# Router and output projection of a two-layer mixture-of-experts trunk: logits in pairs of tiles, the projection's last two tiles in chunk groups, earlier weight requests

## The reference

```
for i in range(2):
    hn = rms_norm(h, norm1_g[i])
    h = h + (rwkv7_time_mix(hn) if i == 0 else conformer_conv(hn))   # each ends in "@ w_o" or "@ w_pw2"
    hn = rms_norm(h, norm2_g[i])
    h = h + hierarchical_moe(hn)
return rms_norm(h, final_g)
```

## Time and profile before

| | us |
|---|---|
| median of 3 runs | 1295.0 (1292.39 to 1297.48) |
| the profiled execution | 1299.55 |
| its span | 1297.5 |
| TensorE busy | 1158.7 (89%) |
| VectorE busy | 526.2 (41%) |
| ScalarE busy | 397.9 (31%) |
| GpSimd busy | 241.0 (19%) |

### The profile page before, as it was taken

How to read it: one execution, slowest core, us unless ns; L and a number is a source line. 1 busy time by engine, 2 the same in 40 slices (tenths; PEclk the granted TensorE clock), 3 DMA queues, 4 the chain that set the end, 5 groups by cost and what they waited for, 6 DMA issues and landing times.

```text
span 1297.5 us, 29460 instructions
## 1 busy us (share of the span) xinstructions
PE 1158.7 (89%) x12654; PEld 626.1 (48%) x12654; DVE 526.2 (41%) x961; ACT 397.9 (31%) x773; POOL 241.0 (19%) x243
## 2 busy tenths in 40 slices
PE   5999999999999989899988877999999899987880
PEld 3355556555555645455544433444444555544440
DVE  6855554554554512411111104699943411111115
ACT  3334445344443322021111113466444111111112
POOL 2000000000000003222211110688801322221110
PEclk8999999999999989899998998999999999999896
DMA  5011101011013072899999976126201699999985
GB/s 167 3 52 60 32 27 53 14 47 39 19 55 134 5 264 82 348 406 424 423 425 427 425 314 260 65 97 278 95 1 38 244 376 424 426 424 427 426 341 218
DMA packets 50209, 271.95 MB, mean 210 GB/s; under 512 B 16386, under 2 KB 19586, under 8 KB 31648
## 3 DMA queue, kind: packets, MB, share of 16 engines
q1 hardware_dynamic: 38048, 240.67, 46.0%
q0 software_dynamic: 10880, 21.00, 4.3%
q10 hardware_dynamic: 1152, 8.39, 1.6%
HBM read 263.73 MB, written 23.07 MB: 221 GB/s over the span
## 4 chain that ended last, share of the span: by engine, by line
PE 62%; DMA 21%; DVE 8%; POOL 4%; issue 2%; ACT 2%; SPq 1%; POOLq 0%; ACTq 0%; DVEq 0%
DMA big<-in_moe_w_gate_up_dram 18%; PE psum L1247 14%; PE psum L820 10%; PE psum L1734 9%; PE psum L1409 6%; PE psum L833 4%; POOL big L1951 4%; DVE psum L2105 2%; PE psum L1979 2%; PE psum L1398 2%; DVE h L924 1%; PE psum L1527 1%; PE psum L799 1%; PE psum L1545 1%; DVE big L431 1%
## 5 line engine op out<-in xcount | busy, mean ns | idle before, releaser
L820 PE MATMUL psum<-big 128*64 128x256 f32 x1728 | 219.5, 399 | 40.9 <-DMA big<-in_moe_w_gate_up_dram 29.7
L1247 PE MATMUL psum<-big 128*128 128x512 f32 x384 | 192.7, 623 | 2.9 <-ACT big L1281 2.2
L820 PEld LDWEIGHTS psum<-big 128*64 128x64 f32 x1728 | 121.4, 141 | 124.1 <-DMA big<-in_moe_w_gate_up_dram 41.2
L895 DVE TENSOR_TENSOR big<-big,psum 128x128 f32<-128x128 f32 x64 | 18.4, 288 | 323.2 <-ACT big L861 323.2
L761 POOL DMA_INDIRECT chosen<-big x64 | 63.7, 995 | 347.0 <-ACT big L871 179.1
L733 POOL TENSOR_SCALAR big<-big 128x1024 f32<-128x1024 f32 x8 | 22.8, 2848 | 566.5 <-PE psum L458 566.4
L833 PE MATMUL psum<-big 128*64 128x512 f32 x512 | 120.9, 593 | 1.2 <-ACT big L866 1.2
L1734 PE MATMUL psum<-big 128*128 128x512 f32 x256 | 115.6, 605 | 0.8 <-ACT big L2074 0.8
L1979 PE MATMUL psum<-big,conv_w 128*128 128x512 f32 x256 | 110.4, 593 | 2.1 <-ACT big L411 1.2
L1951 POOL TENSOR_TENSOR big<-big 128x512 f32<-128x512 f32 x81 | 103.0, 1272 | 42.1 <-ACT big L2053 31.6
L1580 ACT COPY big<-psum 128x512 f32<-128x512 f32 (+1 forms) x112 | 68.3, 648 | 125.1 <-PE psum L1409 122.3
(11 more groups left out here) (260 smaller groups left out, 1341.4 us busy)
## 6 DMA issues: line engine op xcount, KB each, us to landing
big<-in_moe_w_gate_up_dram SPq DMA_DIRECT2D x54, 2048.0 KB, 27.7
big<-in_moe_w_down_dram SPq DMA_DIRECT2D x64, 1024.0 KB, 33.5
conv_w<-in_moe_w_gate_up_dram SPq DMA_DIRECT2D x10, 2048.0 KB, 32.9
big<-in_rwkv_w_rkv_dram SPq DMA_DIRECT2D x24, 512.0 KB, 4.2
conv_w<-in_conv_w_pw_dram SPq DMA_DIRECT2D x8, 1024.0 KB, 4.7
big<-chosen ACTq DMA_DIRECT2D x8, 1024.0 KB, 8.3
big<-in_rwkv_w_o_dram SPq DMA_DIRECT2D x4, 1024.0 KB, 9.1
rows<-big POOLq DMA_DIRECT2D x8, 512.0 KB, 6.0
```

What stands on the lines that cost most here:

```text
L820: last = nc.tensor.matmul(o[half * SLOTS:(half + 1) * SLOTS, 0:F_EXP].rearrange("p (u f) -> p u f", u=2), m.xT[e // 2 % 2][:, c, (e % 2) * ...
L1247: last = nc.tensor.matmul(bank[b], m.w[:, n, c, :], x[:, c, :], start=(c == 0), stop=(c == C - 1))
```

## The change

- **Logits in pairs.** `pe_logits` now takes two tiles at once. Tile 2p writes PSUM partitions 0 to 35 of bank 0, tile 2p+1 partitions 64 to 99 of bank 1, alternating chunk by chunk. Tile 3 goes this way too, and `pe_last_logits` is gone. ScalarE copies the logits of tiles 0, 1 and 2, and DVE those of tile 3. The order on TensorE is columns of tile 2, logits of pair 0, columns of tile 3, flips of pair 0, logits of pair 1, flips of pair 1.
- **Routing in pairs.** DVE runs the steps from scale and bias to the two best experts once for tiles 0 and 1 and once for tiles 2 and 3. The copy into `gl` is gone: the logits tile has four padding columns behind the group logits. The mask's two instructions are one.
- **Moved off DVE's chain.** The shifts for the gates stand behind the tables. Two of the four code products are made by ScalarE (three activations). The rounds are one reduction in place of two steps, and the `rank` update is the last step of `dve_tables`.
- **Rows.** `hn[2]` and `hn[3]` are scaled by ScalarE, between its columns of tile 3 and the copy of tile 2's logits. It also clears `x`. GpSimd scales tiles 0 and 1 and issues all four stores, and reads the rounds before it waits for the stores.
- **Output projection.** Tiles 2 and 3 run in three groups of chunks, (0, 1), (2 to 5) and (6, 7), each first for tile 2, then for tile 3. The columns of tiles 0 and 1 stand behind tile 2's second group. `mix_freed` tells SP when chunks 0 to 1 and 0 to 5 are no longer read.
- **Weight requests.** Layer 0 asks for expert 0's up part right behind expert 3, its down part at the first `mix_freed`, expert 1's up part at the second, and expert 1's down part at the end of the projection. Layer 1 asks for expert 2 at the second `mix_freed`.
- **Expert loop.** `take_rows` is one copy of 1024 columns in place of two of 512, and `pe_stay_busy` writes bank 0. Several semaphores are shared between layers.

```
+        FLIP_BANKS = (4, 6, 5, 7)
         N_LOGITS = N_GRP + N_EXP
 
-        def pe_logits(m, mixer, pe, t):
-
-            pe.wait_ge(m.hnT_ready.sem, m.hnT_ready.by(2 * t + 2))
-            if t == 0:
-                pe.wait_ge(m.params_in, 16 * m.n_params)
+        def logit_rows(t):
+            return slice((t % 2) * 64, (t % 2) * 64 + N_LOGITS)
+
+        def logit_columns(t):
+            return slice((t // 2) * P, (t // 2 + 1) * P)
+
+        def pe_logits(m, mixer, pe, pair):
+
+            if pair == 0:
+                pe.wait_ge(m.params_in.sem, m.params_in.by(16 * m.n_params))
                 pe.wait_ge(mixer.mixed, TT - 1)
-            if t >= 2:
-                pe.wait_ge(m.logitsT_ready.sem, m.logitsT_ready.by(t - 1))
+                pe.wait_ge(m.hnT_ready.sem, m.hnT_ready.by(4))
+            else:
+                pe.wait_ge(m.logitsT_ready.sem, m.logitsT_ready.by(2))
             for c in range(C):
-                last = nc.tensor.matmul(bank[LOGIT_BANKS[t]][0:N_LOGITS, 0:P], m.w_route[:, c, :],
-                                        m.hnT[:, c, t * P:(t + 1) * P], start=(c == 0), stop=(c == C - 1))
+                if pair and c in (0, C // 2):
+                    pe.wait_ge(m.hnT_ready.sem, m.hnT_ready.by(2 * TT - 1 if c == 0 else 2 * TT))
+                for t in (2 * pair, 2 * pair + 1):
+                    last = nc.tensor.matmul(bank[t % 2][logit_rows(t), 0:P], m.w_route[:, c, :],
+                                            m.hnT[:, c, t * P:(t + 1) * P], start=(c == 0), stop=(c == C - 1))
             last.then_inc(m.logitsT_in_psum.sem, 1)
...
+        def pe_flip_logits(m, mixer, pe, pair):
...
+                pe.wait_ge(m.hnT_ready.sem, m.hnT_ready.by(6))
+            pe.wait_ge(m.logitsT_ready.sem, m.logitsT_ready.by(2 * pair + 2))
+            for t in (2 * pair, 2 * pair + 1):
+                nc.tensor.transpose(bank[FLIP_BANKS[t]][:, 0:N_LOGITS], m.logitsT[logit_rows(t), logit_columns(t)],
+                                    ident[logit_rows(t), logit_rows(t)]).then_inc(m.logits_in_psum.sem, 1)
 
         def pe_route_last(m, mixer, pe):
 
             pe_norm_columns(m, pe, TT - 2)
             pe_logits(m, mixer, pe, 0)
+            pe_norm_columns(m, pe, TT - 1)
+            pe_flip_logits(m, mixer, pe, 0)
             pe_logits(m, mixer, pe, 1)
-            pe_norm_columns(m, pe, TT - 1)
-            pe_logits(m, mixer, pe, 2)
-            for t in range(TT - 1):
-                pe_flip_logits(m, mixer, pe, t)
-            pe_last_logits(m, pe)
+            pe_flip_logits(m, mixer, pe, 1)
...
+            act.wait_ge(m.rstd_step.sem, m.rstd_step.by(3 * TT))
+            for t in range(TT // 2, TT):
+                nc.scalar.activation(m.hn[t], m.hn[t], ACT.Copy, scale=m.rstd[:, t:t + 1]).then_inc(m.rows_scaled.sem, 1)
             logits(2)
+            act.wait_ge(m.squares.sem, m.squares.by(TT))
+            for b in range(2):
+                nc.scalar.activation(m.x[b].rearrange("p (c s) -> p c s", c=C), ones[:].unsqueeze(1).broadcast_to([P, C, P]),
+                                     ACT.Copy, scale=0.0).then_inc(m.exp_ready.sem, 1)
...
-            step(nc.vector.tensor_copy(m.gl[:, :, 0:N_GRP], m.logits[:, :, 0:N_GRP]))
...
+            def choose_experts(pair):
+                two, both = (2 * pair, 2 * pair + 1), slice(2 * pair, 2 * pair + 2)
+                dve.wait_ge(m.rstd_step.sem, m.rstd_step.by(3 * (2 * pair + 2)))
+                dve.wait_ge(m.logits_in_psum.sem, m.logits_in_psum.by(2 * pair + 2))
+                for t in two:
+                    last = nc.vector.scalar_tensor_tensor(out=m.logits[:, t, 0:n], in0=bank[FLIP_BANKS[t]][:, 0:n],
+                                                          scalar=m.rstd[:, t:t + 1], in1=m.b_route, op0=ALU.mult,
+                                                          op1=ALU.add)
+                step(last)
+                for t in two:
+                    last = nc.vector.max(m.gmax[:, t, :], m.logits[:, t, N_EXP:])
+                step(last)
+                for t in two:
+                    last = nc.vector.max_index(m.gidx[:, t, :].bitcast(u32), m.gmax[:, t, :], m.logits[:, t, N_EXP:])
+                step(last)
+                step(nc.vector.tensor_copy(m.gidx_f[:, both], m.gidx[:, both, 0].bitcast(u32)))
+                step(nc.vector.tensor_tensor(m.in_group[:, both, :], group_iota[:].unsqueeze(1).broadcast_to([P, 2, N_EXP]),
+                                             m.gidx_f[:, both].unsqueeze(2).broadcast_to([P, 2, N_EXP]), ALU.not_equal))
+                step(nc.vector.scalar_tensor_tensor(out=m.el[:, both, :], in0=m.in_group[:, both, :], scalar=-3.0e38,
+                                                    in1=m.logits[:, both, 0:N_EXP], op0=ALU.mult, op1=ALU.add))
+                if pair == 0:
+                    dve.wait_ge(m.logitsT_in_psum.sem, m.logitsT_in_psum.by(2))
+                    nc.vector.tensor_copy(m.logitsT[logit_rows(TT - 1), logit_columns(TT - 1)],
+                                          bank[1][logit_rows(TT - 1), 0:P]).then_inc(m.logitsT_ready.sem, 1)
+                for t in two:
+                    last = nc.vector.max(m.emax[:, t, :], m.el[:, t, :])
+                step(last)
+                for t in two:
+                    last = nc.vector.max_index(m.eidx[:, t, :].bitcast(u32), m.emax[:, t, :], m.el[:, t, :])
+                step(last)
+
+            for pair in range(2):
...
+                choose_experts(pair)
...
-            step(nc.vector.tensor_tensor(m.gexp, m.logits[:, :, 0:N_GRP], m.gmax[:, :, 0:1].broadcast_to([P, TT, N_GRP]),
-                                         ALU.subtract))
-            step(nc.vector.tensor_tensor(m.ediff, m.emax[:, :, 1], m.emax[:, :, 0], ALU.subtract))
-            assert st.n == GATES_SHIFTED
-
             rhs = m.route_rhs.rearrange("p (t k) n e -> p t k n e", k=2)
-            nc.vector.tensor_tensor(rhs[:, :, :, 0, :], m.pick, token_low[:, 0:2].unsqueeze(1).unsqueeze(3)
-                                    .broadcast_to([P, TT, 2, N_EXP]), ALU.mult)
-            nc.vector.tensor_scalar(rhs[:, :, :, 1, :], m.pick, token_low[:, 2:3], None, ALU.mult)
...
-            dve_slots(m, dve)
+            dve_slots(m, dve, 0, TT)
             dve.wait_ge(m.route, most)
-            step(nc.vector.tensor_scalar(m.over, round_starts[:], m.cmax, None, ALU.is_lt))
-            step(nc.vector.tensor_reduce(m.n_over, m.over, AX.X, ALU.add))
-            nc.vector.tensor_scalar(m.rounds.bitcast(i32), m.n_over, 1.0, None, ALU.add).then_inc(m.rounds_ready, 1)
+            begun = st.done(nc.vector.tensor_scalar(m.over, round_starts[:], m.cmax, None, ALU.is_lt))
+            dve_slots(m, dve, TT, TT * 2)
+            dve.wait_ge(m.route, begun)
+            with nc.allow_low_precision("a count of at most eight rounds"):
+                nc.vector.tensor_reduce(m.rounds.bitcast(i32), m.over, AX.X, ALU.add).then_inc(m.rounds_ready, 1)
             dve_tables(m, dve, 0)
...
+            step(nc.vector.tensor_tensor(m.gexp, m.logits[:, :, groups], m.gmax[:, :, 0:1].broadcast_to([P, TT, N_GRP]),
+                                         ALU.subtract))
+            step(nc.vector.tensor_tensor(m.ediff, m.emax[:, :, 1], m.emax[:, :, 0], ALU.subtract))
+            assert st.n == GATES_SHIFTED
+            dve.wait_ge(m.exp_ready.sem, m.exp_ready.by(ACT_ROUTE))
...
+            rhs = m.route_rhs.rearrange("p (t k) n e -> p t k n e", k=2)
+            act.wait_ge(m.route, PICKED)
+            for k in range(2):
+                nc.scalar.activation(rhs[:, :, k, 0, :], m.pick[:, :, k, :], ACT.Copy, scale=token_low[:, k:k + 1])
+            nc.scalar.activation(rhs[:, :, :, 1, :], m.pick, ACT.Copy, scale=token_low[:, 2:3]
+                                 ).then_inc(m.exp_ready.sem, 1)
...
-            dve.wait_ge(m.hot_ready, TT * 2 * (r + 1))
-            nc.vector.tensor_scalar(m.rank, m.rank, -float(SLOTS), None, ALU.add).then_inc(m.slot_step, 1)
-            dve.wait_ge(m.slot_step, S * r + 1)
...
+            dve.wait_ge(m.hot_ready, TT * 2 * (r + 1))
+            nc.vector.tensor_scalar(m.rank, m.rank, -float(SLOTS), None, ALU.add).then_inc(m.slot_step, 1)
+            dve.wait_ge(m.slot_step, S * r + TABLE_STEPS)
...
+                if t < TT // 2:
+                    pool.wait_ge(m.rstd_step.sem, m.rstd_step.by(3 * t + 3))
+                    pool.wait_ge(m.hnT_in_psum.sem, m.hnT_in_psum.by(t + 1))
+                    nc.gpsimd.tensor_scalar(m.hn[t], m.hn[t], m.rstd[:, t:t + 1], None, ALU.mult).then_inc(m.scaled.sem, 1)
+                    pool.wait_ge(m.scaled.sem, m.scaled.by(t + 1))
+                else:
+                    pool.wait_ge(m.rows_scaled.sem, m.rows_scaled.by(t - TT // 2 + 1))
                 pool.dma_start(rows[m.layer][t * P:(t + 1) * P, :], m.hn[t]).then_inc(m.rows_stored.sem, 16)
-            pool.wait_ge(m.squares.sem, m.squares.by(TT))
-            for b in range(2):
```

(43 more changed lines are left out.)

139 lines of the change are left out of this document (50 added, 89 removed).

## The result

The changed kernel took 1286.1 us in the median of seven runs (1281.3 to 1289.7), the kernel before 1297.5 in seven (1292.4 to 1300.9). The ratio is 0.991, with an interval of 0.989 to 0.993: 11.4 us less. The profiled execution took 1289.67 us with a span of 1287.9, against 1299.55 with 1297.5. The forecast was 1285.9, which is 9.1 us less than 1295.0, the median of the first three runs of the kernel before.

A forecast was written before the change was run, and what follows sets the result against it. Each expert loop was taken as a DMA-bound weight stream whose start, at the first `gate_up`'s end, sets the layer's end. Gains of 6.0 us in layer 0 and 3.1 in layer 1, 9.1 off 1295.0, gave 1285.9; 8-in-10 range 1281 to 1292.5.

The forecast's parts named there:

- up to the gather's issue: Router, projection's end to gather: shorter logits, DVE chain, ranks and tables gain 5.1 us in layer 0, 4.7 in layer 1.
- the gather's landing: Gather to SP's release: early requests empty the weight queue, gaining 0.8 us in layer 0, nothing in layer 1.
- first `gate_up`: First expert's matmuls: both layers run as layer 0 before, nothing in layer 0, a loss of 1.7 us in layer 1.
- Weights that are asked for earlier gain nothing by themselves: Expert weight ring: all of them are in place before the ring turns, so early requests alone gain nothing.
- GpSimd waits for the stores last: Ahead of the gather: last row tile scaled by 522.3, some 10 us before it, so no new wait counted.
- The projection in groups: Output projection: matmuls are moved, none added; cost 0 to 1 us a layer, taken as 0.
- the clock holds in both layers' first `gate_up`: Rival, first expert's matmuls at full clock: 1.7 us more in each layer, 12.5 in all, 1282.5 us; chance 0.20.
- I take 2.0 us for a pair: Router logits on TensorE: two tiles side by side take 2.0 us for 32 records, against 3.6 if serial.
- the pairs don't run side by side: Rival, router logits: TensorE sets the pace, DVE starts 2.4 us later in each layer, 1290.7 us; chance 0.15.
- So DVE starts pair 1 at 523.2: Router, layer 0: ScalarE's chain of 8.4 us after the projection sets DVE's start on the last logits; gain 1.6 us.
- But here a new wait comes.: Picks to ranks' product: five busy matmuls outlast DVE, ranks come 4.85 us after DVE's start, not 4.4; gain 0.5 us.
- From the ranks to the gather, 0.3: Router's end: one step less for the rounds and one less ahead of the tables gain 0.3 us.

The follow-up runs named there:

- the router alone: Changed kernel with the weight requests put back to where they were before, projection still in chunk groups; 1298.2 us, ratio 1.001 to the kernel before.
- the requests alone: Kernel before plus only the projection's last two tiles in chunk groups and the earlier weight requests; 1296.4 us, ratio 1.000.
- the kernel with the other order: Changed kernel with more busy matmuls, DVE copying tile 3's logits after pair 0's experts, ScalarE copying tile 2's between its row scalings; 1285.2 us, ratio 0.990.

## Why the prediction was right, and where it wasn't

The frame held: between the two profiles the streams keep their length to 1 us, and the start sets the end. The terms of the sum, forecast and as the two profiles have them (us gained, layer 0 / 1):

| term | forecast | measured |
|---|---|---|
| up to the gather's issue | 5.1 / 4.7 | 5.70 / 5.54 |
| the gather's landing | 0.8 / 0 | -0.08 / 0.09 |
| one copy | 0.1 / 0.1 | 0.06 / 0.08 |
| first `gate_up` | 0 / -1.7 | -1.24 / 0 |
| start of the stream | 6.0 / 3.1 | 4.44 / 5.71 |

That 1285.9 and 1286.1 lie so close is luck, twice over. The gain was 11.4 us where 9.1 was forecast, and the median of the kernel before, 1295.0 in three runs, was 1297.5 in seven; the two errors cancel. And the layers miss in opposite directions, by 1.6 and 2.6 us, most of it by the clock. One step under the sum was wrong outright, and the router alone shows that it might have cost everything.

**"Weights that are asked for earlier gain nothing by themselves"** and, of the landing, **"In layer 1 nothing".** By themselves, true: the requests alone measured 1.000. But the sum puts them at 0.8 us in layer 0 and zero in layer 1, and the router's terms at 5.1 and 4.7 as if these stood without them. They don't: without the requests the gather is issued at 22.3, a gain of 0.85 and 0.27 us instead of 5.1 and 4.7, and with the clock that follows the two layers together start 3.3 us later than before. Taken away from the finished kernel, the requests cost 4.85 and 5.27 us up to the gather, and 12 us by the median.

**"GpSimd waits for the stores last; ScalarE has scaled the last row tile by 522.3, some 10 us before the gather, so I count no new wait."** The outcome held, with about 1.2 us to spare (landing at 530.2, a microsecond to the issue, gather at 532.44). The reason given didn't carry it: what matters is when the store lands, not when it is issued. Before, it took 10.2 us in layer 0 and 11.1 in layer 1, and this could be had from the DMA view. 522.3 plus 10 is 532.3, just the time of the gather. With the rows stored earlier and the same weights ahead it became 13.9. The text saw the danger for the gather ("Without them the earlier gather would meet the loads") and not for the store ahead of it.

**The projection in groups, cost 0.** The projection's end wanders by more than the 0 to 1 us in question. Groups and requests alone came to a ratio of 1.000 (0.998 to 1.002), so no cost shows.

**The landing in layer 0, 4.42 us against 3.58.** I put the 0.8 us down to the queue of weights. After the change the queue is empty when the gather is issued (share 0.00 just before), and it still takes 4.50 us, in layer 1 3.49. So the term was 0, not 0.8. The two gathers of layer 0 move 0.52 MB, those of layer 1 0.39, before and after, so the difference may go with the bytes; no run changed these alone.

**The clock.** "Nothing in layer 0, a loss of 1.7 in layer 1" was wrong in both. In layer 0 the first `gate_up` took 6.60 us, all but its end at 0.50, a loss of 1.2; in layer 1 it ran at full clock. TensorE's timeline, after, ahead of each:

```profile
537.07 1.16 PE L820 MATMUL psum<-ident,big 128*128 128x128 f32 x8 [2.46 <-DMA big<-rows,big]
539.72 6.60 PE L841 MATMUL psum<-big 128*64 128x256 f32 x32 [1.49 <-DVE big L910]
...
1029.40 1.16 PE L820 MATMUL psum<-ident,big 128*128 128x128 f32 x8 [0.91 <-DMA big<-rows,big]
1032.04 3.67 PE L841 MATMUL psum<-big 128*64 128x256 f32 x32 [1.49 <-DVE big L910]
```

Layer 1's gather lands sooner, so its wait was 0.91 us, not the 1.5 that I counted; layer 0's was 2.46. Even so these two waits alone don't decide it. Before, layer 0 fell to 0.50 behind 0.90 and 1.55 us, some 7 us after an earlier stretch at 0.50 had ended, and layer 1 kept its clock after the change behind 0.91 and 1.49. The two kernels with work given back to GpSimd show it with no earlier fall; layer 1 with the clearing, then with clearing and scaling:

```profile
1026.20 1.16 PE L819 MATMUL psum<-ident,big 128*128 128x128 f32 x8 [0.95 <-DMA big<-rows,big]
1028.86 5.26 PE L840 MATMUL psum<-big 128*64 128x256 f32 x32 [1.49 <-DVE big L909]
```

```profile
1025.07 1.16 PE L813 MATMUL psum<-ident,big 128*128 128x128 f32 x8 [1.03 <-DMA big<-rows,big]
1027.71 3.67 PE L834 MATMUL psum<-big 128*64 128x256 f32 x32 [1.49 <-DVE big L903]
```

What decides between them stays open. The rival "the clock holds in both layers' first `gate_up`" was half true, and the experiment with more busy matmuls is that rival made.

**The logits side by side.** "I take 2.0 us for a pair": 1.95. The restriction that the prediction cites from the Trainium skill, "TensorEngine Tiling (Array Packing)", section Restrictions, that column tiling disables the fast weight load, would have left a pair at 3.6 us only if that loading set the pace. The 1.95 us show that it doesn't here. The rival "the pairs don't run side by side" was priced at 2.4 us a layer and 1290.7 in all; made, it was 3.2 and 1291.5.

**"So DVE starts pair 1 at 523.2".** 522.73, so 2.16 us of gain rather than 1.6. (The terms written down add up to 8.3 us, not 8.4.) The chain through ScalarE was shorter than I summed, and the flips were there before DVE had finished pair 0, which ends at 522.69.

**"But here a new wait comes."** TensorE's ranks were to hold DVE until 4.85 us after its start. They were ready with its last code: 527.18, 4.45 after its start, and no idle time ahead of the product. DVE's own chain set it, so from its start to the ranks 3.6 and 3.2 us were gained where 3.25 was forecast. The wait was 0.1 to 0.2 us away: once DVE started earlier, in the kernel with the other order, the ranks held it.

**From the ranks to the gather, 0.3:** nothing in layer 0 (5.26 against 5.20 us), 0.17 in layer 1.

## What to carry to other kernels

When a chain is shortened, price the next thing that its end waits for by its landing, not by its issue, and read how much slack it had before: here the row stores landed 3.8 and 2.5 us ahead of the gather, and of the 5.5 us that the router had become faster only 0.9 and 0.3 were left without the early requests. What is queued ahead of a small store that somebody waits for belongs in the sum of that chain. Two changes that each measure as nothing can be worth 11 us together, so undo each from the finished kernel as well as trying each alone.

## What the hardware showed that was not expected

- A 512 KB store from GpSimd's queue landed after 3.3 us with nothing queued on SP, and after 5.3, 7.3, 7.9, 10.2, 11.1 or 13.9 us, by how much SP had queued and how soon ahead of it. 6.3 MB at the projection's end held it as long as 8.4 MB did.
- A DVE cast of two columns of SBUF waited out GpSimd's clearing of another tile: 0.84 us instead of 0.17.
- A pair of the 36-column logits, side by side, takes 61 ns a record, and 115 ns when the two tiles share their partitions.
- Nearly the same two waits of TensorE were followed by a granted clock of 0.50 in one kernel (0.95 and 1.49 us) and of 1.00 in another (1.03 and 1.49 us).
